# Order of the input tiles in the first two layers, and the zeros that open the run, in a two-block network kernel

## The reference

```python
for i in range(DEPTH):                                  # DEPTH = 2, these are "layer 0" and "layer 1"
    h = rms_norm(x, norm_mix_w[i])
    proj = jnp.einsum("bld,de->ble", h, w_in[i])
    q, k, v, z, xbc_raw, dt_raw = jnp.split(proj, split_at, axis=-1)
    q = axial_rope(rms_norm(q, q_norm_w[i]), ...)       # 8 heads of 64: four tiles of 128 channels
    k = axial_rope(rms_norm(k, k_norm_w[i]), ...)       # 2 heads: one tile
    attn_out = blocked_gqa(q, k, v)
    ssd_out = ssd_mixer(z, xbc_raw, dt_raw, ...)        # conv and silu of xbc: x (4 tiles), B (2), C (2), then scans
    x = x + jnp.einsum("ble,ed->bld", jnp.concatenate([attn_out, ssd_out], -1), w_out[i])
    h = rms_norm(x, norm_ffn_w[i])
    x = x + jnp.einsum("blf,fd->bld", jax.nn.silu(h @ w_gate[i]) * (h @ w_up[i]), w_down[i])
x = second_block(rms_norm(x, final_norm_w), ...)        # not touched by the change
```

## Time and profile before

| what | value |
|---|---|
| time, median of 3 runs | 2730.93 us (2730.54 to 2733.34) |
| profiled execution, its own time | 2731.48 us |
| its span | 2729.7 us |
| PE busy | 2697.9 us, 99% of the span |
| DVE, ACT busy | 1511.2 us (55%), 1158.5 us (42%) |
| mean granted TensorE clock | 0.998 |

### The profile page before, as it was taken

One profiled execution on the slowest core, in us unless ns is written; L12 is line 12 of the kernel. 1 busy time (PEld: TensorE's weight loads), 2 busy tenths in 40 slices (PEclk: granted clock), 3 DMA queues, 4 the chain that ended last, 5 costly groups with the idle time before them and its releaser, 6 DMA issues.

```text
span 2729.7 us, 33411 instructions
## 1 busy us (share of the span) xinstructions
PE 2697.9 (99%) x13712; PEld 2176.6 (80%) x13712; DVE 1511.2 (55%) x2099; ACT 1158.5 (42%) x1689; POOL 25.6 (1%) x45
## 2 busy tenths in 40 slices
PE   9999999999999999999999999999999999999998
PEld 7767888887767888888888887777777888888886
DVE  6685444345685444344443456878789854544433
ACT  6784322224784322233222234444588453322221
POOL 0000000000000000000000000000000000000000
PEclk9999999999999999999999999999999999999999
DMA  6203323224203333333333342222223332323231
GB/s 220 81 13 100 101 93 101 91 97 145 81 13 101 101 96 97 92 96 99 100 95 95 97 143 85 70 70 63 79 85 99 125 98 93 95 98 98 91 98 61
DMA packets 74344, 256.45 MB, mean 94 GB/s; under 512 B 9040, under 2 KB 10192, under 8 KB 73808
## 3 DMA queue, kind: packets, MB, share of 16 engines
q1 hardware_dynamic: 71680, 241.21, 27.7%
q0 software_dynamic: 2512, 13.11, 1.3%
HBM read 242.22 MB, written 8.39 MB: 92 GB/s over the span
## 4 chain that ended last, share of the span: by engine, by line
PE 91%; ACT 5%; DVE 3%; issue 1%; DMA 0%; SPq 0%; DVEq 0%; ACTq 0%
PE PS L1368 27%; PE PS L1369 26%; PE PS L1370 26%; PE PS L1553 1%; PE PS L1327 1%; PE PS L1390 1%; PE PS L1391 1%; PE PS L1392 1%; PE PS L1520 1%; PE PS L1535 1%; DVE WLO L2028 1%; ACT WHI L1641 1%; ACT PT L1825 1%; ACT DE L1781 0%; PE PS L1499 0%
## 5 line engine op out<-in xcount | busy, mean ns | idle before, releaser
L1368 PE MATMUL PS<-HHI,WHI 128*128 128x512 f32 x2288 | 912.7, 399 | 0.0
L1370 PE MATMUL PS<-HHI,WLO 128*128 128x512 f32 x2288 | 891.7, 390 | 0.0
L1369 PE MATMUL PS<-HLO,WHI 128*128 128x512 f32 x2288 | 891.1, 389 | 0.0
L2028 DVE TENSOR_TENSOR WLO<-WR,WHI 128x1024 fp32r<-128x1024 f32 (+2 forms) x446 | 536.0, 1204 | 517.2 <-ACT WHI L1641 513.8
L1641 ACT CAST WHI<-WR 128x1024 fp32r<-128x1024 f32 (+2 forms) x446 | 457.5, 1027 | 345.6 <-PE PS L1370 322.4
L1368 PEld LDWEIGHTS PS<-HHI,WHI 128*128 128x128 f32 x2288 | 429.6, 188 | 102.2 <-issue 13.0
L1369 PEld LDWEIGHTS PS<-HLO,WHI 128*128 128x128 f32 x2288 | 429.8, 188 | 90.2 <-issue 5.0
L1370 PEld LDWEIGHTS PS<-HHI,WLO 128*128 128x128 f32 x2288 | 429.5, 188 | 90.2
L1368 PE MATMUL PS<-FHI,WHI 128*128 128x512 f32 x704 | 274.3, 390 | 0.0
L1369 PE MATMUL PS<-FLO,WHI 128*128 128x512 f32 x704 | 273.9, 389 | 0.0
L1370 PE MATMUL PS<-FHI,WLO 128*128 128x512 f32 x704 | 273.9, 389 | 0.0
(11 more groups left out here) (330 smaller groups left out, 2537.1 us busy)
## 6 DMA issues: line engine op xcount, KB each, us to landing
WR<-in_stream SPq DMA_DIRECT2D x413, 512.0 KB, 3.4
WR<-in_stream SPq DMA_DIRECT2D x32, 384.0 KB, 3.0
xkeep<-X POOLq DMA_DIRECT2D x3, 2048.0 KB, 9.1
X<-xkeep POOLq DMA_DIRECT2D x24, 256.0 KB, 5.1
ROT<-RQ SPq DMA_DIRECT2D x40, 64.0 KB, 2.0
X<-in_xin SPq DMA_DIRECT2D x8, 256.0 KB, 7.6
out<-X SPq DMA_DIRECT2D x8, 256.0 KB, 2.2
KD<-RQ SPq DMA_DIRECT2D x8, 128.0 KB, 3.6
```

The source lines that it names most:

```text
L1368: e.matmul(out, hi[:, i, :], xhi, start=first, stop=False)
L1369: e.matmul(out, hi[:, i, :], xlo, start=False, stop=False)
L1370: t = e.matmul(out, lo[:, i, :], xhi, start=False, stop=final)
L2028: e.tensor_tensor(lo, raw, hi.bitcast(F32), ALU.subtract).then_inc(S["dve_low"], 1)
```

## The change

Two edits. The order of the 13 tiles of both layers is changed: C tiles 16 and 17 come ahead of query tiles 2 and 3. And DVE writes the zeros as its first instruction, ahead of its wait for the first vector load, while PE multiplies three full products of zeros where there were three and a half.

```diff
-IN_ORDER = (4, 0, 10, 11, 12, 13, 14, 15, 1, 2, 3, 16, 17)
+IN_ORDER = (4, 0, 10, 11, 12, 13, 14, 15, 1, 16, 17, 2, 3)
...
         q.wait_ge(S["dve_warm"], 1)
-        for columns_ in (T, T, T, T // 2):
-            e.matmul(PS[7][:, 0:columns_], WARM[:, 0:P], WARM[:, 0:columns_], start=True, stop=True)
+        for _ in range(3):
+            e.matmul(PS[7][:, :], WARM[:, 0:P], WARM[:, :], start=True, stop=True)
...
     def vector_engine(e):
         q = Waits(e)
+        e.memset(WARM[:, :], 0.0).then_inc(S["dve_warm"], 1)
...
         q.wait_ge(s_head, 16)
-        e.memset(WARM[:, :], 0.0).then_inc(S["dve_warm"], 1)
```

## The result

| | before | after |
|---|---|---|
| time, median of 3 runs | 2730.93 us | 2748.91 us (2746.85 to 2749.75) |
| span of the profiled execution | 2729.7 | 2747.1 |
| mean granted TensorE clock | 0.998 | 0.994 |

The ratio is 1.0063, 95% interval 1.005 to 1.0077: 18 us slower, where the forecast was 6 and the range ended at 2742.

The account below looks back on a forecast made before the run. No engine alone bounds the tails: three nearly full in-order queues (PE, DVE, ACT) wait on each other. Terms 0 + 0 + 6.0 = +6.0 on the profiled 2731.48 gave 2737.5, 2737.0 us on the median; 8-in-10 range 2731.5 to 2742.

Parts of the forecast that it names:

- The start: Start of the kernel: first matmul group comes sooner, the second still waits for its inputs until 9.64; 0 us.
- The clock rival: Behind the zeros at the start: PE falls back to 1.2 GHz after a pause; +2.5 us, 2739.5; chance 0.18.
- End of the stream: Both layers: a rope chain behind the last query tile delays `rcs` to 762.0; +0.5 us in layer 0.
- The running sums: Tail, behind `rcs`: DVE works from 762.0 without a pause for 18.8 us, so they are done at 780.8.
- Rest of layer 0: Layer 0's tail after the first decays: decays set the pace, end at 831.1 as before; 0 us.
- Rest of layer 1: Layer 1's tail: second decays late, the scan's DVE work has no cover; +6.0 us taken between +4.6 and +7.2.
- The full count: Rest of layer 1's tail with 0.2 us for each step between engines: end at 838.3 against 831.10, +7.2.
- the lower bound: Rest of layer 1's tail counted without the 0.2 us per step between engines: +4.6.
- the second decays behind the last `qk`: Layer 1's tail: second chunk's decays found no four free banks; attention is done early, the scan left alone.
- place 3: Late in layer 1's tail: `zout`, `w`, `goff`, `xc` in DVE's run without a pause, 21.1 us from 810.8 to 831.9.
- rows 4 and 5: Profile rows near the program's end: a pause of 2.17 us, then a granted clock of 0.52, the 1.2 GHz level.
- a pause of 3 to 4 us at 760 to 767: Each tail: PE waits for `st` while DVE waits for the rope's DMAs ahead of `rcs`.

Follow-up runs that it names:

- all_mended: Changed kernel with five products of zeros, products of constants in seven PE pauses of the tails, and GpSimd's first `ya` after the last running sum: 2740.7 us.
- goff_late: all_mended with layer 1's third-chunk `goff` behind the last `xc` and 11 instead of 23 products of constants ahead of the last `yt`: 2740.7 us.
- fill_half: Changed kernel with PE making products of constants before six waits in the tails, half as many as in a first try: 2746.1 us.
- layer0_new: Changed kernel with the new tile order in layer 0 only, the old order in layer 1: 2735.0 us.
- mended_decays1: all_mended with layer 1's second decays placed one `qk` behind the first, and products of constants there in two pauses only: 2741.9 us.

## Why the prediction was wrong

Point by point. L1 stands for layer 1, in us behind its fifth `qk`:

| station in L1 | predicted | after | all_mended |
|---|---|---|---|
| `rcs` after the rope's DMAs | 26.6 | 27.1 | 27.1 |
| running sums done | 45.4 | 49.2 | 47.7 |
| first decays' exponentials done | 53.1 | 56.3 | 54.1 |
| second decays | 67.6 | 71.0 | 68.8 |
| last `xc` done | 96.5 | 100.5 | 98.3 |
| held output row | 102.9 | 109.3 | 105.0 |

The held row is the fourth of the product; in before it stood 95.8 behind `qk`.

- **The start: right, and the rival with it.** 0 was −0.3 in the profile, because the second group came 0.5 sooner, with its DMAs, and not for the zeros' sake. The clock rival (0.18) did not happen there, but did in three of nine executions, at 1.5 instead of 2.5.
- **End of the stream: right up to `rcs`,** 0.5 off, with DVE idle 3.2 us in both tails and PE waiting for `stadd`, as announced. **The running sums came late:** 3.8 in L1; in layer 0 they ended at 169.50, that is 169.50 − 121.81 = 47.7 behind its fifth `qk`, 2.3 later than the same 45.4. Of L1's, 1.5 is GpSimd's `ya`, a step that the change moved as well and that I did not list (it waits for the last `st`; the prediction names every queue but GpSimd's), and 1.6 a wait of DVE for ACT's `yv`, which the count of DVE's work alone left out.
- **Rest of layer 0: right.** Free of clock and GpSimd +0.6 where 0 to 0.5 was said. With them +3.7.
- **Rest of layer 1: direction and place right, size not.** The full count gave 102.9 and the mended kernel has 105.0; then I took 6.0 instead of the counted 7.2, for the lower bound's sake. Both of these are small: 9.1 against 6.0. The cause I gave, the second decays behind the last `qk`, holds for 5.9 us, with all that it moves behind it. The run of DVE work at the end, place 3, exists as described; undoing it brought the held row 1.5 us forward, of the 2.9 that its `yt` gained (goff_late).
- **The step that failed:** the clock. I read rows 4 and 5, a pause of 2.17 and half clock behind it, and applied them at the start only. In the same text I forecast a pause of 3 to 4 us at 760 to 767 in each tail, and 12 us of idle PE in the rest of L1, and priced none of them. Keeping PE busy through the pauses gave back 1.7 in layer 0 and 2.5 in L1 by itself (fill_half). With GpSimd's first `ya`, which I had nowhere, they are the 8.2 us between 2740.7 and 2748.9: 3.1 in layer 0, 4.8 in L1. Of the 12 us between forecast and result 8.2 are these two, 3.1 is layer 1's order and 0.6 layer 0's.

The range ended at 2742 because it was built of the counted terms and their rivals. Every missing term found here had the same sign.

## What to carry to other kernels

Where a change opens a pause of PE near 2 us or more, or two or three of about 1 us close together, add a chance of a fall with its price: here 1.6 us, and about twice as much behind the pauses of 3 and 5 us where PE restarts with small work. Do so everywhere and not only at the start. When an edit makes a step earlier and the time doesn't move, look whether the longer pause in front of the next step brought a fall: goff_late lost its 1.5 us that way. List the steps of every engine that the change moves, GpSimd's too, and ask what DVE does beside them. And when two engines are slowed at the same moment, remove both before calling either harmless.

## What the runs showed of the hardware that was not expected

- The same pause of 2.28 us in the same list was followed by matmuls at 1.2 GHz in after and not in layer0_new; between full tiles 2.22 us did it three times in eight, 1.85 us five times, and single pauses of 1.48 us or less never in 24.
- The clock column shows it: 0.50 to 0.72 in windows of 4 to 9 us, while the mean over the kernel moved from 0.998 to 0.994 only.
- The Trainium skill (TensorE: Matmul & The Clock Gate, Part 1: The HAM clock gate) calls the array slow by default and released by activity. The zeros at the start agree (loads of 0.34, later 0.19 us); so do the falls behind pauses.
- A product of two constants of 128x128 in float32 takes 0.225 us on PE, a transposition of the same size 0.11.
- An SBUF by SBUF multiplication on DVE beside GpSimd's two products lasted until they were over: 2.32, 2.22 against 0.68 us. Where DVE began first, both were slowed in all_mended (1.42 against 1.04 us on GpSimd, 2.13 against 1.28 for two pieces on DVE); in mended_decays1 the same meeting left `w` as fast as ever and stretched GpSimd's product to 3.23.
